# Channel-major projections of a two-block network: matmuls of 512 and 256 columns issued two and two over two blocks

## The chip, the cores and the metric

The kernel is one program on one core of a Trainium2 chip. The metric is the device time of one execution in microseconds, taken as the median of several runs; lower is better.

## The reference, cut to what matters

Two transformer-like blocks work on 256 tokens of width 2048 in float32. The first has gated recurrence and attention heads and a gated feed-forward net of width 5632 with a short convolution; the second has two layers with pooling, block attention, and attention into 256 memory tokens. Nearly all of the arithmetic lies in the projections, each a product of activations with a weight matrix:

```python
proj = h @ w_in[l]                                        # 2048 x 7176
x = x + jnp.concatenate([o_a, o_b], axis=-1) @ w_out[l]   # 2048 x 2048
x = x + (jax.nn.silu(conv(h @ w_gate)) * (h @ w_up)) @ w_down
mk, mv = jnp.split(mem @ w_mem_kv, 2, axis=-1)
k, v = jnp.split(h @ w_kv, 2, axis=-1)
u = h @ w_in[i]
y = mixed @ w_out[i]
pooled_mixed = jnp.einsum('bsgc,gcd->bsgd', pooled, pool_w)
```

## The kernel before

**Split operands.** Each float32 operand is split in two: a high part, rounded to TensorE's faster 32-bit format (fp32r), and a low part, the rest. A projection is the sum of high weight times high activation, high weight times low activation, and low weight times high activation. Activations lie as `[128, blocks of 128 channels, 2, 256 tokens]`, high beside low, in `ahl` (most projections), `hhl` (feed-forward down), `memhl` (memory), `fox_span` (half of the first output projection) and `phl` (pooling).

**Weight tiles.** Each projection is a phase: a number of chunks, each of `tpc` weight tiles. SP loads a tile (mostly 1 MB) into one of four `raw` buffers; ScalarE writes its high part into one of three slots of `hl_ring` (`hi`, L337) and VectorE its low part (`lo`, L340), two tiles ahead of TensorE. TensorE waits for a tile's low part (`lo_ready`), issues all its matmuls, and the last one raises `tile_used`, which frees the slot.

**Form A, channel-major.** The weights are the stationary operand, 128 by 128. For each block of 128 input channels there are two matmuls into the same bank of the accumulator `G`: L386 has the high weights and all 512 columns (high and low activations side by side), L387 has the low weights and the 256 columns of the high activations. Each has a weight load of its own. A chunk owns a pair of banks of `G`, one bank (512 float32) for each of two blocks of 128 output channels. A standard tile (`std_mats`) holds eight input blocks for both output blocks: 16 pairs of matmuls, the eight of output block 0 first, then the eight of block 1. A tile of the down projection (`down_mats`) has one output block and eleven input blocks; one of the pooling projection (`pool_mats`) has one output block and three.

**Form F, token-major.** The activations are stationary, the weights stream with 512 columns, and three matmuls (L391, L392, L393) of 512 columns follow one another. The diff does not alter what they issue. A further matmul stream stands at L881: the forget gate's projection, 48 matmuls of 256 columns, each with its own weight load.

**What sets the order.** The program is written engine by engine. `pe_phase` walks over chunks and tiles. `between` puts other work (transposes, attention heads, recurrence) behind a tile. VectorE and ScalarE read `G` when a chunk's last tile is done, and free the pair of banks with `pair_free`.

Of the kernel before, what the change touches and what calls it, by code (L numbers as in the profile page):

```python
# [25 lines left out]
P = 128  # L26
TOK = 256
# [37 lines left out]
def program(nc, A):  # L65
    ctx = ExitStack()
    with ctx:
# [44 lines left out]
        hi, lo = hl_ring[:, :, 0, :], hl_ring[:, :, 1, :]  # L112
# [40 lines left out]
        G = ctx.enter_context(nc.psum_tensor("G", [P, 4, 512], F32))  # L153
# [161 lines left out]
        order = list(phases.values())  # L315
# [39 lines left out]
        def no_evict(c):  # L355
            pass

        def pe_phase(eng, name, between=None, norm=None, halves=None):


            p = phases[name]
            xhl = p.rhs
            for c in range(p.chunks):
                pair = (p.chunk0 + c) % 2
                for t in range(p.tpc):
                    m = c * p.tpc + t
                    n = p.tile0 + m
                    s = n % RINGS
                    eng.wait_ge(lo_ready, n + 1)
                    if norm is not None and c == 0:  # L370
                        eng.wait_ge(n_lo, 4 * norm + (t + 1) * (4 // p.tpc))
                    if halves is not None and c == 0:
                        for ready, count in halves[t]:
                            eng.wait_ge(ready, count)
                    if t == 0 and p.chunk0 + c >= 2:
                        eng.wait_ge(pair_free[pair], (p.chunk0 + c) // 2)
                    if name.startswith("down") and c == 0 and t < 2:
                        eng.wait_ge(h_lo, HB // 2 * int(name[-1]) + (6 if t == 0 else 11))
                    last = None
                    for b, ks, width, col, first, final in p.mats(c, t):  # L380
                        bank = 2 * pair + b
                        for q, (kt, k) in enumerate(ks):
                            st, sp = first and q == 0, final and q == len(ks) - 1
                            if p.form == "A":
                                w = slice(kt * width + col, kt * width + col + P)
                                eng.matmul(G[:, bank, :], hi[:, s, w], xhl(k), start=st, stop=False)  # L386
                                last = eng.matmul(G[:, bank, 0:TOK], lo[:, s, w], xhl(k)[:, 0, :], start=False, stop=sp)  # L387
                            else:
                                w = slice(kt * width, (kt + 1) * width)
                                tok = slice(b * P, (b + 1) * P)  # L390
                                eng.matmul(G[:, bank, :], xhl(k)[:, 0, tok], hi[:, s, w], start=st, stop=False)  # L391
                                eng.matmul(G[:, bank, :], xhl(k)[:, 0, tok], lo[:, s, w], start=False, stop=False)  # L392
                                last = eng.matmul(G[:, bank, :], xhl(k)[:, 1, tok], hi[:, s, w], start=False, stop=sp)  # L393
                    last.then_inc(tile_used, 1)
                    if between is not None:
                        between(m)
# [432 lines left out]
        def _(pe):  # L829
# [25 lines left out]
            def x_transposes(m):  # L855
# [4 lines left out]
                for g in range(3 * m - 3, min(3 * m, 8)):  # L860
                    transposes(xtok, g)

            pe_phase(pe, "mem_k0", between=x_transposes)
            pe.wait_ge(vec_loaded, 11 * 16)
            pe.wait_ge(x_ready, 5)
            for v, n in enumerate((124, 105, 88)):
                last = pe.transpose(XP[0][:, v * P:v * P + n], vrows[0:n, v, :], ident[0:n, 0:n])
            last.then_inc(vec_t, 1)
            pe.wait_ge(x_ready, 8)
            pe_phase(pe, "mem_v0")  # L870
            pe_norm(pe, 0)
            for n in ("mem_k1", "mem_v1"):
                pe_phase(pe, n)
# [797 lines left out]
```

## Time and profile before

| | us |
|---|---|
| median of 3 runs | 2169.74 |
| lowest, highest | 2167.94, 2171.20 |
| the profiled execution | 2165.34 |
| its span, first to last instruction | 2163.6 |

The profile shows one execution. Its busy table gives each engine's time and share of the span. The chain that ended last is followed back from the last instruction. Groups of instructions are named by line, engine and operation with the tensors that they write and read. The timeline lists instructions by start time. A table of stretches counts the instructions of one line in given stretches of the span. PE is TensorE's matmul side, PEld its weight loads, DVE VectorE, ACT ScalarE. The mean granted TensorE clock is 0.979 of full speed.

### The profile page before, as it was taken

Reading aid. Unit: us, or ns where it says so; the run is one execution under the profiler, and the core shown is the slowest. Engines: PE = TensorE matmul, PEld = TensorE weight load, DVE = VectorE, ACT = ScalarE, POOL = GpSimd, SP = SyncE. Lnnn points to the kernel's source line nnn. Section 1 sums busy time; section 2 is a strip of 40 time slices with the busy share of each in tenths; the row PEclk is TensorE's granted clock in tenths of the full one; section 3 lists DMA queues with packets and bytes.
Section 4 is the critical chain, followed back from the end, with each engine's and each line's share of the span. In section 5 each row is a group of like instructions: output and inputs, shape, how many; then the busy total and the mean of one; then the engine's idle time right before and its main releaser. Section 6 shows DMA issues by size and latency. Waiting matters only on the chain.

```text
span 2163.6 us, 26132 instructions
## 1 busy us (share of the span) xinstructions
PE 2065.9 (95%) x11431; PEld 1787.2 (83%) x11431; DVE 1282.9 (59%) x1136; ACT 882.4 (41%) x785; POOL 32.2 (1%) x54
## 2 busy tenths in 40 slices
PE   7999999999799999999999997999889699999996
PEld 6888898888688888888888886888678588888885
DVE  4556555456666665556666555577576653566664
ACT  5435434444444443334444334333343334344532
POOL 1000000000000000000000000000000200000001
PEclk9999999999999999999999999999999899999998
DMA  8565544445445555675555666556175355654551
GB/s 276 175 219 189 172 140 156 156 137 175 156 156 195 195 194 149 186 224 181 194 178 178 163 185 192 156 176 199 40 230 185 97 188 181 189 155 138 195 195 59
DMA packets 381261, 373.38 MB, mean 173 GB/s; under 512 B 6526, under 2 KB 351419, under 8 KB 380123
## 3 DMA queue, kind: packets, MB, share of 16 engines
q1 hardware_dynamic: 379744, 365.19, 53.7%
q0 software_dynamic: 944, 6.36, 0.8%
q8 instruction: 90, 1.47, 0.3%
q10 hardware_dynamic: 459, 0.16, 0.0%
q14 instruction: 24, 0.20, 0.0%
HBM read 367.49 MB, written 4.19 MB: 172 GB/s over the span
## 4 chain that ended last, share of the span: by engine, by line
PE 92%; DVE 4%; ACT 1%; issue 1%; DMA 0%; POOL 0%; SPq 0%; DVEq 0%; ACTq 0%
PE G L386 49%; PE G L387 25%; PE G L391 4%; PE G L392 4%; PE G L393 4%; PE SB L605 2%; PE TB L503 1%; DVE hl_ring L340 1%; PE OB L626 1%; DMA raw<-in_w_mem_kv 0%; DVE xres L560 0%; ACT hl_ring L337 0%; DVE scr L401 0%; PE OB L629 0%; PE TB L881 0%
## 5 line engine op out<-in xcount | busy, mean ns | idle before, releaser
L386 PE MATMUL G<-ahl,hl_ring 128*128 128x512 f32 x3648 | 1293.3, 399 | 38.0 <-issue 31.9
L340 DVE TENSOR_TENSOR hl_ring<-raw,hl_ring 128x2048 fp32r<-128x2048 f32 (+2 forms) x372 | 787.5, 2121 | 520.6 <-ACT hl_ring L337 519.2
L387 PE MATMUL G<-ahl,hl_ring 128*128 128x256 f32 x3648 | 1023.7, 281 | 0.0
L337 ACT ACTIVATE hl_ring<-raw 128x2048 fp32r<-128x2048 f32 (+2 forms) x372 | 659.8, 1777 | 635.9 <-PE G L387 518.9
L386 PEld LDWEIGHTS G<-ahl,hl_ring 128*128 128x128 f32 x3648 | 688.8, 189 | 204.9 <-issue 36.1
L387 PEld LDWEIGHTS G<-ahl,hl_ring 128*128 128x128 f32 x3648 | 692.0, 190 | 0.4 <-issue 0.2
L386 PE MATMUL G<-hhl,hl_ring 128*128 128x512 f32 x704 | 248.8, 399 | 0.0
L387 PE MATMUL G<-hhl,hl_ring 128*128 128x256 f32 x704 | 197.7, 281 | 0.0
L386 PEld LDWEIGHTS G<-hhl,hl_ring 128*128 128x128 f32 x704 | 132.3, 188 | 33.0
L387 PEld LDWEIGHTS G<-hhl,hl_ring 128*128 128x128 f32 x704 | 133.0, 189 | 0.0
L391 PE MATMUL G<-hl_ring,ahl 128*128 128x512 f32 x256 | 100.2, 392 | 0.0
L393 PE MATMUL G<-hl_ring,ahl 128*128 128x512 f32 x256 | 99.7, 389 | 0.0
L392 PE MATMUL G<-hl_ring,ahl 128*128 128x512 f32 x256 | 99.7, 389 | 0.0
L401 DVE TENSOR_REDUCE arena<-G 128x512 f32<-128x1024 f32 x58 | 70.9, 1222 | 41.4 <-PE G L387 41.3
L1162 ACT ACTIVATE cbuf<-gsum,convp 128x256 f32<-128x256 f32 x44 | 24.1, 595 | 108.4 <-DVEq L1467 108.4
L641 ACT ACTIVATE ringscr<-SB,nmax 128x256 f32<-128x256 f32 (+1 forms) x48 | 20.2, 426 | 114.5 <-DVE nmax L662 114.5
L1168 ACT ACTIVATE hhl<-hv 128x512 fp32r<-128x512 f32 x22 | 13.9, 633 | 111.6 <-DVE hv L1483 111.6
L393 PEld LDWEIGHTS G<-hl_ring,ahl 128*128 128x128 f32 x256 | 48.1, 188 | 10.0
L391 PEld LDWEIGHTS G<-hl_ring,ahl 128*128 128x128 f32 x256 | 48.1, 188 | 9.8
L392 PEld LDWEIGHTS G<-hl_ring,ahl 128*128 128x128 f32 x256 | 48.1, 188 | 9.7
L386 PE MATMUL G<-memhl,hl_ring 128*128 128x512 f32 x128 | 47.1, 410 | 5.4 <-DVE hl_ring L340 5.4
L386 PE MATMUL G<-fox_span,hl_ring 128*128 128x512 f32 x128 | 45.7, 399 | 0.0
(306 smaller groups left out, 1499.7 us busy)
## 6 DMA issues: line engine op xcount, KB each, us to landing
raw<-in_w_in SPq DMA_DIRECT2D x120, 1024.0 KB, 5.5
raw<-in_w_out SPq DMA_DIRECT2D x48, 1024.0 KB, 5.4
raw<-in_w_ffn_gate SPq DMA_DIRECT2D x44, 1024.0 KB, 5.0
raw<-in_w_ffn_up SPq DMA_DIRECT2D x44, 1024.0 KB, 5.1
raw<-in_w_ffn_down SPq DMA_DIRECT2D x64, 704.0 KB, 4.9
raw<-in_w_kv_shared SPq DMA_DIRECT2D x24, 1024.0 KB, 5.1
raw<-in_w_mem_kv SPq DMA_DIRECT2D x16, 1024.0 KB, 7.7
raw<-in_pool_w SPq DMA_DIRECT2D x12, 192.0 KB, 2.5
```

What stands on the lines that cost most here:

```text
L337: eng.activation(hi[:, s, 0:size], raw[:, r, 0:size], ACT.Copy).then_inc(hi_ready, 1)
L340: eng.tensor_tensor(lo[:, s, 0:size], raw[:, r, 0:size], hi[:, s, 0:size].bitcast(F32), ALU.subtract).then_inc(lo_ready, 1)
L386: eng.matmul(G[:, bank, :], hi[:, s, w], xhl(k), start=st, stop=False)
L387: last = eng.matmul(G[:, bank, 0:TOK], lo[:, s, w], xhl(k)[:, 0, :], start=False, stop=sp)
L391: eng.matmul(G[:, bank, :], xhl(k)[:, 0, tok], hi[:, s, w], start=st, stop=False)
L392: eng.matmul(G[:, bank, :], xhl(k)[:, 0, tok], lo[:, s, w], start=False, stop=False)
L393: last = eng.matmul(G[:, bank, :], xhl(k)[:, 1, tok], hi[:, s, w], start=False, stop=sp)
L401: return eng.tensor_reduce(dst, g, AX.X, ALU.add)
L503: last = eng.matmul(TB[:, 0:TOK], meanw[:, :], normt[:, k, :], start=k == 0, stop=k == KT - 1)
L605: last = eng.matmul(o_, l_, r_, start=m == 0, stop=m == len(mm) - 1)
L626: eng.matmul(OB[:, 0:256], H.v(h, 0), pt[:, 0:256], start=True, stop=False)
L1162: act.activation(cbuf[:, b, :], gsum[:, b, :], ACT.Identity, scale=convp[:, f, 2:3], bias=convp[:, f, 3:4]).then_inc(conv_c, 1)
```

## The change

In form A the loop over output blocks outside and input blocks inside is replaced by one list. With two output blocks in the tile the list goes over the input blocks outside and the two output blocks inside; with one it goes over the input blocks. The list is taken two entries at a time: first the two L386 kinds (512 columns, high weights), then the two L387 kinds (256 columns, low weights). Where the list has an odd length (down: 11, pool: 3), the last entry stands alone. The number of matmuls and loads, their operands and the waits are the same. Form F is untouched.

```diff
+        def alternate(eng, p, pair, s, c, t):
+
+            mats = p.mats(c, t)
+            last = None
+            if len(mats) == 2:
+                order = [(mats[b], q) for q in range(len(mats[0][1])) for b in (0, 1)]
+            else:
+                order = [(mats[0], q) for q in range(len(mats[0][1]))]
+            for g in range(0, len(order), 2):
+                for (b, ks, width, col, first, final), q in order[g:g + 2]:
+                    kt, k = ks[q]
+                    w = slice(kt * width + col, kt * width + col + P)
+                    eng.matmul(G[:, 2 * pair + b, :], hi[:, s, w], p.rhs(k), start=first and q == 0, stop=False)
+                for (b, ks, width, col, first, final), q in order[g:g + 2]:
+                    kt, k = ks[q]
+                    w = slice(kt * width + col, kt * width + col + P)
+                    last = eng.matmul(G[:, 2 * pair + b, 0:TOK], lo[:, s, w], p.rhs(k)[:, 0, :], start=False,
+                                      stop=final and q == len(ks) - 1)
+            return last
+
...
-                    for b, ks, width, col, first, final in p.mats(c, t):
+                    if p.form == "A":
+                        last = alternate(eng, p, pair, s, c, t)
+                    for b, ks, width, col, first, final in p.mats(c, t) if p.form != "A" else ():
                         bank = 2 * pair + b
                         for q, (kt, k) in enumerate(ks):
                             st, sp = first and q == 0, final and q == len(ks) - 1
-                            if p.form == "A":
-                                w = slice(kt * width + col, kt * width + col + P)
-                                eng.matmul(G[:, bank, :], hi[:, s, w], xhl(k), start=st, stop=False)
-                                last = eng.matmul(G[:, bank, 0:TOK], lo[:, s, w], xhl(k)[:, 0, :], start=False, stop=sp)
-                            else:
+                            if p.form == "F":
                                 w = slice(kt * width, (kt + 1) * width)
```

## Rows read from the trace of the kernel before

**Rows 1.** Page, busy time: engine, busy us, share of span, instructions.
```profile
PE 2065.9 (95%) x11431; PEld 1787.2 (83%) x11431; DVE 1282.9 (59%) x1136; ACT 882.4 (41%) x785; POOL 32.2 (1%) x54
```
**Rows 2.** Page, chain that ended last: shares of the span by line.
```profile
PE G L386 49%; PE G L387 25%; PE G L391 4%; PE G L392 4%; PE G L393 4%; PE SB L605 2%; PE TB L503 1%; DVE hl_ring L340 1%; PE OB L626 1%; DMA raw<-in_w_mem_kv 0%; DVE xres L560 0%; ACT hl_ring L337 0%; DVE scr L401 0%; PE OB L629 0%; PE TB L881 0%
```
**Rows 3.** Waits of TensorE: who for whom, us in total, times, longest.
```profile
PE G L386 <- DVE hl_ring L340: 14.0, 5, 5.4
```
**Rows 4.** TensorE groups: out<-in, shape, count | busy, mean ns | idle before.
```profile
L386 PE MATMUL G<-ahl,hl_ring 128*128 128x512 f32 x3648 | 1293.3, 399 | 38.0 <-issue 31.9 <-DVE hl_ring L340 4.1 <-DVE ahl L1549 1.7
L387 PE MATMUL G<-ahl,hl_ring 128*128 128x256 f32 x3648 | 1023.7, 281 | 0.0
L386 PE MATMUL G<-hhl,hl_ring 128*128 128x512 f32 x704 | 248.8, 399 | 0.0
...
L386 PE MATMUL G<-memhl,hl_ring 128*128 128x512 f32 x128 | 47.1, 410 | 5.4 <-DVE hl_ring L340 5.4
L386 PE MATMUL G<-fox_span,hl_ring 128*128 128x512 f32 x128 | 45.7, 399 | 0.0
...
L386 PE MATMUL G<-pooledhl,hl_ring 128*128 128x512 f32 x36 | 15.7, 463 | 6.9 <-DVE hl_ring L340 4.5 <-DVE arena L1523 2.4
```
**Rows 5.** Timeline, TensorE, from 300.02 us: start us, duration us, instruction.
```profile
300.02 0.39 PE L386 MATMUL G<-ahl,hl_ring 128*128 128x512 f32 x1
300.25 0.27 PE L387 MATMUL G<-ahl,hl_ring 128*128 128x256 f32 x1
300.36 0.40 PE L386 MATMUL G<-ahl,hl_ring 128*128 128x512 f32 x1
...
303.83 0.40 PE L386 MATMUL G<-ahl,hl_ring 128*128 128x512 f32 x1
```
**Rows 6.** Timeline, TensorE, from 1000.00 us.
```profile
1000.00 0.40 PE L386 MATMUL G<-ahl,hl_ring 128*128 128x512 f32 x1
1000.23 0.28 PE L387 MATMUL G<-ahl,hl_ring 128*128 128x256 f32 x1
1000.35 0.40 PE L386 MATMUL G<-ahl,hl_ring 128*128 128x512 f32 x1
...
1004.24 0.40 PE L386 MATMUL G<-ahl,hl_ring 128*128 128x512 f32 x1
```
**Rows 7.** Stretches, L386 alone: length, PE and PEld busy (count), clock, DMA share, GB/s.
```profile
133.00:210.00 77.00, 77.00 (x219) 40.96 (x218) 1.00 0.63 205
...
478.00:582.00 104.00, 101.90 (x288) 53.99 (x288) 1.00 0.58 189
601.00:842.00 241.00, 241.00 (x696) 130.31 (x695) 1.00 0.56 182
846.00:1334.00 488.00, 488.00 (x1383) 259.51 (x1382) 1.00 0.63 189
1360.00:1534.00 174.00, 174.00 (x494) 92.51 (x493) 1.00 0.55 169
1593.00:1675.00 82.00, 82.00 (x238) 44.26 (x237) 1.00 0.60 193
1713.00:1772.00 59.00, 59.00 (x172) 31.86 (x171) 1.00 0.63 206
1843.00:1892.00 49.00, 49.00 (x140) 26.01 (x140) 1.00 0.64 193
```
**Rows 8.** Timeline, TensorE, token-major form, first and last of twelve matmuls.
```profile
229.94 0.39 PE L391 MATMUL G<-hl_ring,ahl 128*128 128x512 f32 x1
...
232.43 0.39 PE L393 MATMUL G<-hl_ring,ahl 128*128 128x512 f32 x1
```
**Rows 9.** Timeline, TensorE, gate projection, first and last of 22 matmuls.
```profile
211.92 0.40 PE L881 MATMUL TB<-ahl,fwhi 128*128 128x256 f32 x2
...
214.44 0.28 PE L881 MATMUL TB<-ahl,fwhi 128*128 128x256 f32 x1
```
**Rows 10.** Timeline, TensorE's weight loads, at 300.02 us.
```profile
300.02 0.19 PEld L387 LDWEIGHTS G<-ahl,hl_ring 128*128 128x128 f32 x1
```

## The prediction

> **What bounds the kernel now.** I read the busy table first. TensorE is busy for 95% of the span, VectorE, the next engine, for 59% [rows 1]. The chain that ended last says the same: 49% and 25% of the span go to the two matmul lines that the change reorders, L386 (512 columns) and L387 (256 columns), and none of the lines of another engine that it lists reaches 2% [rows 2]. The waits of TensorE agree: its largest wait on another engine for these matmuls is for the low half of a weight tile, 14.0 us in five waits over the whole span [rows 3]. So nothing but the distance from one matmul's start to the next sets most of the time, and a nanosecond saved on each lands in the end almost whole.
>
> There are 3648 + 704 + 128 + 128 + 36 = 4644 pairs of one L386 and one L387 [rows 4]. The mean durations in those rows (399 and 281 ns) are no price: matmuls overlap, and a duration holds the pipeline's latency. What counts is start to start, so I went to the timeline.
>
> **Two paces of the same pair.** From 300.02 to 303.83 us there are 11 pairs: 3.81 / 11 = 346.4 ns a pair, some 230 ns from the 512 to the 256 and some 115 ns back to the next 512 [rows 5]. From 1000.00 to 1004.24 us the same two lines take 4.24 / 12 = 353.3 ns a pair [rows 6]. Which pace holds is a matter of the stretch, and it persists. I read stretches in which hardly anything but these pairs runs, each length divided by its number of matmuls (weight loads, one fewer where a matmul is cut by the edge) [rows 7]. The granted clock is 1.00 in all eight, the full level of 2.4 GHz, so the clock is not what differs: 241 us / 695 = 346.8 ns, 82 / 237 = 346.0 and 59 / 171 = 345.0 are the quick pace; 77 / 218 = 353.2, 488 / 1382 = 353.1, 174 / 493 = 352.9, 104 / 288 (with 2 us idle, 101.9 / 288 = 353.8) and 49 / 140 = 350.0 are the slow one. (An edge is worth one pair, which blurs the short ones.) The difference is 353.1 - 346.8 = 6.3 ns by the two long stretches and 6.9 ns by the two timelines; I take 6.6 ns and call it a step.
>
> The slow stretches hold 219 + 1383 + 494 + 288 + 140 = 2524 pairs, the quick ones 696 + 238 + 172 = 1106. The remaining 1014 lie between transposes and attention matmuls; I put half of them, 507, to the slow pace (my choice, the timeline shows both there). That makes 3031 slow pairs, 65% of all, and 3031 x 6.6 ns = 20.0 us in steps. This is all that a reordering can win if the quick pace is the floor.
>
> Is it? Where matmuls of one size follow one another, each with a weight load of its own, the rows show one pace only. The token-major form of 512 columns: 229.94 to 232.43 us, 11 distances, 226.4 ns [rows 8]. The gate projection of 256 columns: 211.92 to 214.44 us, 21 distances, 120.0 ns [rows 9]. Their sum is 346.4 ns, exactly the quick pair. So the quick pace is the sum of the two kinds, and the step appears in mixed streams only.
>
> **The change, part by part.** It removes and adds no instruction: 4644 matmuls of each kind, the same loads, the same operands, waits and increments, on one core. Only TensorE's order within a weight tile changes, from 512, 256, 512, 256 to 512, 512, 256, 256 over the two output blocks.
>
> (a) New neighbours. 512 after 512: 226.4 ns by rows 8; 256 after 256: 120.0 ns by rows 9. One 512 to 256 and one 256 to 512 stay: 230 to 235 and 115 to 120 ns [rows 5, 6]. Four matmuls come to 226.4 + 120.0 + 346.4 = 692.8 ns at the quick pace and 226.4 + 120.0 + 353.3 = 699.7 ns at the slow one, against 692.8 and 706.6 ns now. Nothing is won where the pace is quick; one step of two is won where it is slow.
>
> (b) How many size changes are left. Tiles with two blocks: (4644 - 704 - 36) / 2 = 1952 groups of four. The down projection has one block and 11 matmul pairs a tile (704 / 11 = 64 tiles), taken two by two with one left over: 6 changes for 11, so 384. Pool: 12 tiles of three, 24. Together 2360 for 4644. At today's slow share, 0.65 x 2360 = 1540 steps stay and 3031 - 1540 = 1491 go: 1491 x 6.6 ns = 9.8 us.
>
> (c) Weight loads. In the trace a load starts with the matmul before the one it serves: one is at 300.02 us, with the matmul of 300.02 [rows 5, 10]. Now a load under a 256 serves a 512; afterwards one load in four lies under a 256 and serves a 256. Two 256s in a row with a load each are what rows 9 show at 120.0 ns, so the term is 0 in (a). Bounds: the quick pair's 256 takes about 115 ns, so -5 ns; above, a full step, +6.6 ns on each of 2322 groups, 15 us. I take 0, the nearest row being the same kind of operation.
>
> (d) Accumulator banks. Successive matmuls now write different banks. Today a tile changes bank once, after 8 pairs. The tile of rows 5 ends soon after 303.83, so its change falls near 301.4, within the 11 pairs whose mean is 346.4 ns: no cost seen, and the 11 distances of rows 8 in one bank are no cheaper. I take 0; upper bound one step per matmul pair again.
>
> (e) Other engines. A tile's last matmul still releases it and both banks of a chunk are still released together, so SP's transfers, ScalarE's high halves and VectorE's low halves keep their order. A tile of 16 pairs takes 16 x 0.3533 = 5.65 us of TensorE and would take some 5.60; VectorE at 59% has room for that. The cover of the weight tiles stays.
>
> [...]
>
> Sum: -9.8 us. The profiled execution took 2165.3 us, of which 1.7 lie outside its span; the median of the runs shown is 2169.7, 4.4 us more. I take the 9.8 off the median: 2159.9 us, -0.45%.
>
> **The rivals.** Count steps per group of four; today it is 3031 / 2322 = 1.3.
> - Forecast: the step belongs to a size change and keeps its share, 0.65 per group. 2159.9 us. For: one-size streams show none. Chance 0.34.
> - All gone: the step needs the strict alternation to hold itself, and the new pattern settles at the quick pace everywhere. -20.0 us, 2149.7 us. For: the paces last for hundreds of us, like a rhythm that locks, and a new rhythm might not lock. Against: no row shows a mixed stream in fours. Chance 0.20.
> - Order is indifferent: the step comes once per pair or its like, whatever the neighbours, or every group takes exactly one. 0 us (2169.7) in the first case, 2322 x 6.6 = 15.3 in place of 20.0, so -4.7 us (2165.0), in the second. For: the quick pair is a plain sum. Chance 0.26.
> - Slower: the new rhythm locks in the slow pace everywhere, two steps a group, the second one at the 256 that follows a 256 into another bank, where a load and a change of bank fall together in the shortest slot, some 0.12 us. (4644 - 3031) x 6.6 = +10.6 us, 2180.4 us. It decides from 1.3 steps a group on. For: after short interruptions today's stream falls into the slow pace more often than not, five of the eight stretches in the table [rows 7]. Against: rows 9. Chance 0.20.
>
> **How the numbers follow.** The predicted time is the forecast's, 2159.9 us. About 0.2% (4.3 us) is what a measurement of this kernel can tell from no change. Forecast and "all gone" are faster, 0.54. The case of -4.7 us lies on that bound and I count it with "order is indifferent", 0.26. With a little of the slower case that is too small to be told, within 0.2% comes to 0.27 and slower to 0.19. For 8 in 10 the range starts at the case "all gone" with 1.7 us beyond for the choice of 507, 2148, and runs through the forecast (alone: 2155 to 2164) and the indifferent order into two thirds of the slower case, 2177.
>
> **What would show it.** Timeline after: two L386 starts 0.23 us apart, then 0.23, then 0.12, 0.12; groups of four at 0.693 or 0.700 us, not 0.707. Long stretches of such groups, length over number of L386: 346.4 to 350 ns. If all stretches read 346.7, "all gone" holds; if 353, the rhythm locked slow; if a mixture of 346.7 and 353.3 stays with the old share, order is indifferent. In (c), a distance of 256 to 256 well over 120 ns would refute the load term; in (d), 512 to 512 over 227 ns the bank term. What makes the prediction wrong otherwise: the down projection or the stretches between attention matmuls choosing another pace than today, which is worth up to 507 x 6.6 = 3.3 us here.

## The result and the profile after

The changed kernel takes 2155.07 us (median of 4 runs, 2154.10 to 2156.07) against 2169.36 us before in the same comparison: ratio 0.9934, 95% interval 0.9916 to 0.9951. That is 14.3 us less, where 9.8 us were forecast. The profiled execution took 2154.1 us with a span of 2152.4 us, 11.2 us less than the span before.

The page of the changed kernel, busy time, then the chain that ended last by line:

```profile
PE 2052.7 (95%) x11431; PEld 1779.1 (83%) x11431; DVE 1282.6 (60%) x1136; ACT 882.2 (41%) x785; POOL 32.2 (1%) x54
...
PE G L370 49%; PE G L374 24%; PE G L409 4%; PE G L411 4%; PE G L410 4%; PE SB L623 2%; PE TB L521 1%; DVE hl_ring L340 1%; PE OB L644 1%; ACT hl_ring L337 0%; DVE xres L578 0%; DVE scr L419 0%; PE TB L899 0%; DVE arena L501 0%; PE OB L647 0%
```

L370 and L374 are the old L386 and L387. Counts, the other engines' busy times and the chain's make-up are those of [rows 1, 2]; TensorE alone has become shorter. Its largest wait on another engine for these matmuls has not moved either (14.0 us in [rows 3]):

```profile
PE G L370 <- DVE hl_ring L340: 14.7, 5, 5.0
```

So the gain lies between the starts of the matmuls. The timeline of TensorE in the changed kernel, same place as [rows 6] (a line with x2 is two matmuls, start of the first and length of both):

```profile
1000.16 0.63 PE L370 MATMUL G<-ahl,hl_ring 128*128 128x512 f32 x2
1000.63 0.39 PE L374 MATMUL G<-ahl,hl_ring 128*128 128x256 f32 x2
1000.86 0.63 PE L370 MATMUL G<-ahl,hl_ring 128*128 128x512 f32 x2
...
1005.73 0.40 PE L370 MATMUL G<-ahl,hl_ring 128*128 128x512 f32 x1
```

Eight groups of four from 1000.16 to 1005.73 us: 5.57 / 8 = 0.696 us, or 348.1 ns per pair. Before it was 353.3 here and 346.4 in the stretches of [rows 5]. The stretches agree; L370 alone, length, PE and PEld busy with counts, clock, DMA share, GB/s:

```profile
133.00:210.00 77.00, 69.39 (x223) 33.65 (x222) 1.00 0.65 205
478.00:575.00 97.00, 87.32 (x278) 42.23 (x279) 1.00 0.61 195
601.00:842.00 241.00, 217.28 (x694) 105.34 (x692) 1.00 0.58 183
1000.00:1200.00 200.00, 180.32 (x575) 87.39 (x575) 1.00 0.57 183
```

Each length is divided by the mean of its two counts: 97 / 278.5 = 348.3, 241 / 693 = 347.8, 200 / 575 = 347.8, 77 / 222.5 = 346.1 ns per pair, with an uncertainty of one or two pairs at the edges, since matmuls of one size now come in twos (for the shortest stretch that is 1.6 to 3.1 ns). What was slow (133, 478, 1000) and what was quick (601) now run at one pace, close to 348.1. The two paces of the old kernel have become one, some 1.5 ns above its quick one and 5 ns below its slow one.

### The profile page after: what moved, and what is told of

It reads as the page before. It is cut to its first block, busy times and chain, and to the rows that moved or that the text cites. A ratio compares the mean times of both kernels' runs of the same rounds, so it can differ in the third digit from the quotient of the medians.

```text
span 2152.4 us, 26132 instructions
## 1 busy us (share of the span) xinstructions
PE 2052.7 (95%) x11431; PEld 1779.1 (83%) x11431; DVE 1282.6 (60%) x1136; ACT 882.2 (41%) x785; POOL 32.2 (1%) x54
## 4 chain that ended last, share of the span: by engine, by line
PE 93%; DVE 4%; ACT 2%; issue 1%; POOL 1%; DVEq 0%; ACTq 0%; POOLq 0%
PE G L370 49%; PE G L374 24%; PE G L409 4%; PE G L411 4%; PE G L410 4%; PE SB L623 2%; PE TB L521 1%; DVE hl_ring L340 1%; PE OB L644 1%; ACT hl_ring L337 0%; DVE xres L578 0%; DVE scr L419 0%; PE TB L899 0%; DVE arena L501 0%; PE OB L647 0%
## 5 line engine op out<-in xcount | busy, mean ns | idle before, releaser
L370 PE MATMUL G<-ahl,hl_ring 128*128 128x512 f32 x3648 | 1156.7, 399 | 38.8 <-issue 31.9
L374 PEld LDWEIGHTS G<-ahl,hl_ring 128*128 128x128 f32 x3648 | 689.3, 189 | 163.5
L374 PE MATMUL G<-ahl,hl_ring 128*128 128x256 f32 x3648 | 720.2, 279 | 0.0
L370 PEld LDWEIGHTS G<-ahl,hl_ring 128*128 128x128 f32 x3648 | 559.8, 190 | 41.9 <-issue 35.7
L370 PE MATMUL G<-hhl,hl_ring 128*128 128x512 f32 x704 | 223.5, 395 | 0.0
L374 PEld LDWEIGHTS G<-hhl,hl_ring 128*128 128x128 f32 x704 | 132.3, 188 | 28.6
L374 PE MATMUL G<-hhl,hl_ring 128*128 128x256 f32 x704 | 144.0, 279 | 0.0
L370 PEld LDWEIGHTS G<-hhl,hl_ring 128*128 128x128 f32 x704 | 109.8, 189 | 2.7
L370 PE MATMUL G<-memhl,hl_ring 128*128 128x512 f32 x128 | 42.3, 413 | 5.0 <-DVE hl_ring L340 5.0
L419 DVE TENSOR_REDUCE hv<-G 128x512 f32<-128x1024 f32 x22 | 26.9, 1225 | 30.3 <-PE G L374 30.3
```

The lines of the kernel that those rows point to most:

```text
L370: eng.matmul(G[:, 2 * pair + b, :], hi[:, s, w], p.rhs(k), start=first and q == 0, stop=False)
L374: last = eng.matmul(G[:, 2 * pair + b, 0:TOK], lo[:, s, w], p.rhs(k)[:, 0, :], start=False, stop=final and q == len(ks) - 1)
L419: return eng.tensor_reduce(dst, g, AX.X, ALU.add)
```

## The experiments

The table has the kernels that were executed six or ten times, each with its own spread. The kernel before stands once for each comparison. The other kernels below were executed once. All code edits are cut to the lines that matter (`...`).

| kernel | runs | median us | lowest to highest | ratio to before, 95% interval |
|---|---|---|---|---|
| before, with the first four | 31 | 2167.16 | 2153.62 to 2172.30 | |
| twos in one bank | 10 | 2154.32 | 2152.45 to 2157.29 | 0.9951 (0.9934 to 0.9969) |
| alternating sizes, banks in turn | 10 | 2163.65 | 2154.89 to 2174.41 | 0.9988 (0.9963 to 1.0013) |
| fours | 10 | 2164.16 | 2163.15 to 2165.58 | 1.0002 (0.9981 to 1.0022) |
| whole tile | 10 | 2153.87 | 2152.22 to 2155.07 | 0.9961 (0.9943 to 0.9980) |
| before, with the next two | 19 | 2166.04 | 2153.98 to 2173.03 | |
| one group of twos, then alternating | 10 | 2170.05 | 2168.01 to 2171.82 | 1.0024 (1.0003 to 1.0044) |
| skewed | 10 | 2173.16 | 2171.42 to 2175.00 | 1.0031 (1.0016 to 1.0047) |
| before, with the last | 11 | 2165.71 | 2154.19 to 2171.58 | |
| tiles turned | 6 | 2150.14 | 2148.51 to 2150.97 | 0.9933 (0.9908 to 0.9957) |

**Sizes or banks?** The change does two things at once: it puts equal sizes side by side, and it lets successive matmuls write different banks. Two kernels do one alone. The first keeps the groups of four but takes them within one output block:

```diff
-            if len(mats) == 2:
-                order = [(mats[b], q) for q in range(len(mats[0][1])) for b in (0, 1)]
-            else:
-                order = [(mats[0], q) for q in range(len(mats[0][1]))]
+            order = [(mat, q) for mat in mats for q in range(len(mat[1]))]
...
```

> Edit: the groups of four (512, 512, 256, 256) are kept, but taken over two input blocks of one output block, so that all four write one bank; banks change once per tile, as before the change. Theory S (the order of the sizes sets the pace): as the changed kernel, ratio 0.993 to 0.994, some 348.4 ns per pair everywhere. Theory B (the gain comes from writing two banks in turn): the old two paces, 346.7 and 353.3 ns, ratio 0.999 to 1.001.

Measured: 2154.32 us, the changed kernel's time. Its timeline has five groups of four from 1099.90 to 1103.38 us, 3.48 / 5 = 0.696 us each:

```profile
1099.90 0.39 PE L371 MATMUL G<-ahl,hl_ring 128*128 128x256 f32 x2
1100.13 0.62 PE L367 MATMUL G<-ahl,hl_ring 128*128 128x512 f32 x2
...
1103.38 0.40 PE L371 MATMUL G<-ahl,hl_ring 128*128 128x256 f32 x2
```

The second alternates the sizes as before and alternates the banks with each pair:

```diff
...
-            for g in range(0, len(order), 2):
+            for g in range(0, len(order), 1):
...
```

Each slice `order[g:g + 2]` becomes `order[g:g + 1]`; in the kernels below it grows with the step in the same way.

> Edit: sizes alternate 512, 256, 512, 256 as before the change, but the two output blocks take turns pair by pair, so that the bank changes with each pair. Theory S: ratio 0.998 to 1.002, two paces of 346.7 and 353.3 ns as before. Theory B: ratio about 0.994 and one pace near 348.4 ns.

Measured: 2163.65 us, not told apart from before; the interval of the ratio, 0.9963 to 1.0013, leaves out the 0.994 of theory B. Both old paces are there, but they have changed places; L367 alone, in stretches:

```profile
133.00:210.00 77.00, 76.89 (x222) 41.62 (x222) 1.00 0.65 205
...
601.00:842.00 241.00, 241.00 (x683) 128.15 (x682) 1.00 0.57 180
```

241 / 682 = 353.4 ns where [rows 7] have the quick pace, and 77 / 222 = 346.8 ns where they have the slow one. Theory S holds against theory B: the order of the sizes does it, and no effect of the banks is seen. That the same phases have the other pace in this kernel also shows that the pace doesn't belong to a phase's own weights and activations.

**Do fewer size changes help further?**

```diff
-            for g in range(0, len(order), 2):
+            for g in range(0, len(order), 4):
...
```

> Edit: four matmuls of 512 columns, then four of 256, over two input blocks and two output blocks. Theory S1 (each change of size carries a fixed share of a step; 3.3 ns per group in the changed kernel): 2 x 693.3 + 3.3 ns per eight, 347.5 ns per pair, 4 us less than the changed kernel, ratio about 0.9915. Theory L (each order of sizes locks into a pace of its own, with no rule by the number of changes): any pace between 346.7 and 353.3 ns.

Measured: 2164.16 us, 9 us more than in twos. Groups of eight in its timeline:

```profile
1100.49 1.09 PE L367 MATMUL G<-ahl,hl_ring 128*128 128x512 f32 x4
1101.42 0.63 PE L371 MATMUL G<-ahl,hl_ring 128*128 128x256 f32 x4
...
1104.69 1.09 PE L367 MATMUL G<-ahl,hl_ring 128*128 128x512 f32 x4
```

Three groups in 4.20 us: 350.0 ns per pair in this stretch. Half as many size changes cost more, so theory S1, a fixed share of a step at each change, is refuted. The spread, 2.4 us over ten executions, is small like the changed kernel's. With threes:

> Edit, on the changed kernel: three matmuls of 512 columns, then three of 256, over two output blocks. If the cost grows steadily from twos (348.4 ns per pair) to fours (350.8): 349 to 350 ns, device time 2157 to 2162 us. Theory L without a rule: any pace from 346.7 to 353.3.

Measured: 2164.52 us (one run), above the 2157 to 2162 expected from a steady rise. Three matmuls of 512 and three of 256 take 1.04 to 1.07 us, never twice the same, and a single pair stands at the end of a tile of 16:

```profile
1101.19 0.88 PE L367 MATMUL G<-ahl,hl_ring 128*128 128x512 f32 x3
...
1105.41 0.86 PE L367 MATMUL G<-ahl,hl_ring 128*128 128x512 f32 x3
```

Twelve pairs in 4.22 us are 351.7 ns each. With all of a tile's matmuls of one size in a row:

```diff
-            for g in range(0, len(order), 2):
+            for g in range(0, len(order), 16):
...
```

> Edit: all matmuls of 512 columns of a weight tile (16; 11 in the down projection), then all of 256. One change of size each way per tile. Theory S1: 346.4 to 346.9 ns per pair, 7 to 8 us less than the changed kernel, ratio about 0.990. Theory L: any pace between 346.7 and 353.3 ns; the token-major phases and the gate projection, streams of one size, ran at 226.4 and 120.0 ns, and if these hold here as well the stretches are 16 x 226.4 and 16 x 120.0 ns long.

Measured: 2153.87 us, 1.2 us under the changed kernel's 2155.07 (whose runs are from another comparison), not 7 to 8. Its timeline shows where the rest went:

```profile
1001.27 3.82 PE L367 MATMUL G<-ahl,hl_ring 128*128 128x512 f32 x16
1004.93 2.08 PE L371 MATMUL G<-ahl,hl_ring 128*128 128x256 f32 x16
1006.84 3.82 PE L367 MATMUL G<-ahl,hl_ring 128*128 128x512 f32 x16
```

A tile takes 5.57 us, 348.1 ns a pair. The sixteen 512s take 3.66 us, where 16 x 226.7 is 3.63 (226.7 ns is the distance in the run with one size only, below; [rows 8] give 226.4); the sixteen 256s take 1.91 us, where 16 x 120.0 is 1.92. The seventh 512 of the tile starts here:

```profile
1002.66 0.39 PE L367 MATMUL G<-ahl,hl_ring 128*128 128x512 f32 x1
```

The first six distances take 1.39 us, 232 ns each, and the ten behind them 2.27 us, 227 ns each. So long runs of one size do settle at the paces of [rows 8, 9], and what a tile takes above them lies in the first 512s after 256s.

**Is it the weight load under the short matmul?** Two kernels change the length of the low-weight matmul in the kernel before.

```diff
-                                last = eng.matmul(G[:, bank, 0:TOK], lo[:, s, w], xhl(k)[:, 0, :], start=False, stop=sp)
+                                g2 = G[:, bank, :].rearrange("p (h t) -> p h t", h=2)[:, :, 0:192]
+                                last = eng.matmul(g2, lo[:, s, w], xhl(k)[:, :, 0:192], start=False, stop=sp)
```

> Edit, on the kernel before: the low-weight matmul streams 384 columns (192 tokens of the high and of the low activations) in place of 256; order 512, 384, 512, 384. It leaves out 64 tokens of the low-weight product and adds a low-times-low term. Theory W (the step is a weight load that doesn't quite fit under a matmul of 256 columns): one pace, (512 + 384) / 2.4 + 2 x 13.3 = 400.0 ns per pair in all stretches. Theory L (a rhythm of the order of sizes, whatever is loaded): more than one pace or one off 400.0 by a step of 6.7 ns or a part of it.

Measured: 2440.34 us. There are two paces, 4.07 / 10 = 407.0 ns per pair around 150 us and 4.13 / 10 = 413.0 ns around 1100 us, and neither is 400.0. (The 400.0 is an estimate: no run has 384 columns alone, and 173.3 ns lie halfway between 120.0 for 256 and 226.7 for 512.)

```profile
149.96 0.39 PE L386 MATMUL G<-ahl,hl_ring 128*128 128x512 f32 x1
150.19 0.34 PE L388 MATMUL G<-ahl,hl_ring 128*128 128x384 f32 x1
...
154.03 0.39 PE L386 MATMUL G<-ahl,hl_ring 128*128 128x512 f32 x1
...
1099.86 0.40 PE L386 MATMUL G<-ahl,hl_ring 128*128 128x512 f32 x1
1100.09 0.34 PE L388 MATMUL G<-ahl,hl_ring 128*128 128x384 f32 x1
...
1103.99 0.40 PE L386 MATMUL G<-ahl,hl_ring 128*128 128x512 f32 x1
```

The stride of those operands could have been the cause, so it was repeated with contiguous columns:

```diff
...
+                                    last = eng.matmul(G[:, bank, 0:384], lo[:, s, w],
+                                                      xhl(k).rearrange("p h t -> p (h t)")[:, 0:384], start=False, stop=sp)
```

> Edit, on the kernel before: the low-weight matmul streams 384 contiguous columns (the high activations of 256 tokens, then the low ones of 128), in place of 256; in the first output projection it stays at 256. It adds part of the low-times-low term. It repeats the run with 192 + 192 columns without its stride. If the stride made the two paces there (406.7 and 413.3 ns): 400.0 ns. If the two sizes did: 406.7 and 413.3 again.

Measured: 2430.51 us, with both paces again: ten pairs from 149.73 to 153.80 us, 407 ns each, and ten from 1099.63 to 1103.77 us, 414 ns each:

```profile
149.73 0.39 PE L386 MATMUL G<-ahl,hl_ring 128*128 128x512 f32 x1
...
153.80 0.39 PE L386 MATMUL G<-ahl,hl_ring 128*128 128x512 f32 x1
...
1099.63 0.40 PE L386 MATMUL G<-ahl,hl_ring 128*128 128x512 f32 x1
...
1103.77 0.40 PE L386 MATMUL G<-ahl,hl_ring 128*128 128x512 f32 x1
```

The stride is not the cause. A load under 384 columns has some 53 ns more than one under 256, and the two paces are still there, 6 to 7 ns apart. Theory W as the cause of the step is refuted. The other direction:

```diff
+                                n2 = TOK if sp else P
+                                last = eng.matmul(G[:, bank, 0:n2], lo[:, s, w], xhl(k)[:, 0, 0:n2], start=False, stop=sp)
```

> Edit, on the kernel before: the low-weight matmul streams 128 columns (half the tokens; the other half of the low-weight product is left out, except in the last matmul of a block); order 512, 128. Theory W: the load that stands under the 128 shows in full, and the distance after it stays at 113 to 120 ns, so that a pair takes 340 to 350 ns and nothing is won. Theory L: loads are not the limit, (512 + 128) / 2.4 + 2 x 13.3 = 293.3 ns per pair, give or take a step of 6.7.

Measured: 2121.19 us, 49 us less than the 2169.98 us that the kernel before took beside it (one execution each). TensorE's matmuls and loads:

```profile
1049.74 0.44 PE L386 MATMUL G<-ahl,hl_ring 128*128 128x512 f32 x1
1050.02 0.22 PE L388 MATMUL G<-ahl,hl_ring 128*128 128x128 f32 x1
1050.02 0.19 PEld L386 LDWEIGHTS G<-ahl,hl_ring 128*128 128x128 f32 x1
1050.08 0.44 PE L386 MATMUL G<-ahl,hl_ring 128*128 128x512 f32 x1
1050.13 0.19 PEld L388 LDWEIGHTS G<-ahl,hl_ring 128*128 128x128 f32 x1
1050.36 0.22 PE L388 MATMUL G<-ahl,hl_ring 128*128 128x128 f32 x1
1050.36 0.19 PEld L386 LDWEIGHTS G<-ahl,hl_ring 128*128 128x128 f32 x1
...
1051.44 0.44 PE L386 MATMUL G<-ahl,hl_ring 128*128 128x512 f32 x1
```

Five pairs in 1.70 us, 340 ns. Half of the columns of the low matmul are gone (53 ns, half of what a 512 takes more than a 256), and the pair is only 6 ns shorter than the quick pair of [rows 5], 13 ns shorter than the slow one. By the loads the pair divides into 0.11 us (1050.02 to 1050.13) and 0.23 us (1050.13 to 1050.36); 340 - 226.7 is 113 ns. The matmuls start otherwise: the 128 comes 0.28 us after the 512 and the next 512 only 0.06 us after the 128. So the least that a short matmul adds to the pair is some 113 ns, and the rhythm of the loads says that the load is the limit; that reading is argued from these rows, since no run has the short matmul without its load. W is right about the floor, which lies just under the 120 ns of a matmul of 256, and wrong about the step. Only one pace was seen here; L386 alone, in a stretch, gives 200 / 587.5 = 340.4 ns:

```profile
1000.00:1200.00 200.00, 200.00 (x588) 109.97 (x587) 1.00 0.59 186
```

The Trainium skill, page "TensorE: Matmul & The Clock Gate", section "LDWEIGHTS (loading the stationary operand)", gives a load as its columns over 1.2 GHz, by estimate 107 ns for these 128; the 113 ns lie 6 ns above it.

**One size only.**

```diff
-                                last = eng.matmul(G[:, bank, 0:TOK], lo[:, s, w], xhl(k)[:, 0, :], start=False, stop=sp)
+                                last = eng.matmul(G[:, bank, :], lo[:, s, w], xhl(k), start=False, stop=sp)
```

> Edit, on the kernel before: the low-weight matmul streams all 512 columns (it adds the low-times-low term). Only one size is left in these stretches. All theories by which the step needs two sizes: 2 x 226.7 = 453.3 ns per pair, everywhere, in one pace. If the step belongs to the channel-major form itself (these weights, these operands), a second pace of 460 ns appears.

Measured: 2637.04 us; seven starts, six distances in 1.36 us, 226.7 ns each (the matmuls of 512 columns in both lines):

```profile
1050.05 0.39 PE L386 MATMUL G<-hhl,hl_ring 128*128 128x512 f32 x1
...
1051.41 0.39 PE L386 MATMUL G<-hhl,hl_ring 128*128 128x512 f32 x1
```

No second pace of 460 ns per pair shows in the stretches that were read. The step needs two sizes; the channel-major form has none of its own.

**What picks the pace of an alternating stretch?** The times of the kernel before range over 19 us, from 2153.62 to 2172.30 in 31 executions, while every kernel in groups stays within 5 us. The kernel with alternating sizes and banks in turn ranges over 19.5 us. The clock doesn't explain it: the three shortest of all its executions (2153.62 to 2153.98 us) and the three longest (2172.02 to 2173.03 us) have mean granted clocks of 0.978 to 0.980 alike. Nor does the traffic of transfers tell the paces apart: [rows 7] have the quick one at 182 to 206 GB/s and the slow one at 169 to 205. If each execution picks its paces anew at the interruptions, a fixed start for each tile should narrow the range. Two kernels do that; the first begins each tile with one group of twos and then alternates:

```diff
+            plan = [(False, 0), (False, 1), (True, 0), (True, 1)]
+            plan += [(low, i) for i in range(2, len(order)) for low in (False, True)]
...
```

> Edit, on the changed kernel: only the first four matmuls of each weight tile go 512, 512, 256, 256; the other 14 pairs alternate 512, 256 (output blocks in turn). The question is what picks the pace of an alternating stretch. Theory P (a disturbance at the stretch's start picks it, and it then holds): every tile starts alike, so all tiles of one kind have one pace, and the time varies from run to run much less than that of the kernel before. If it is the quick one, 346.7 to 347.1 ns per pair and 2147 to 2150 us, better than both kernels; if the slow one, 353 ns and some 2175 us. Theory N (the pace is set by something outside TensorE's stream): both paces as before, ratio 0.999 to 1.001.

The second starts with two of 512, alternates 512 and 256, and ends with two of 256:

```diff
+            plan = [(False, 0)]
+            for i in range(1, len(order)):
+                plan += [(False, i), (True, i - 1)]
+            plan.append((True, len(order) - 1))
...
```

> Edit, on the changed kernel: a tile starts with two of 512, then 256 and 512 alternate, and it ends with two of 256. Theory P: again one pace for all tiles, and little variation from run to run; quick 2147 to 2150 us, slow some 2175 us. Theory N: both paces, ratio 0.999 to 1.001.

Measured: 2170.05 us within 3.8 us, and 2173.16 us within 3.6 us, at the top of the range of the kernel before. L376 and L378 alone, 1000 to 1200 us; the first row is that of the seeded kernel,

```profile
1000.00:1200.00 200.00, 197.54 (x568) 104.20 (x567) 1.00 0.58 186
```

the second that of the skewed one:

```profile
1000.00:1200.00 200.00, 197.28 (x567) 103.97 (x566) 1.00 0.59 186
```

200 / 567.5 = 352.4 and 200 / 566.5 = 353.0 ns: the slow pace, and in the first the timeline from 1061.14 to 1064.67 us (ten pairs, 353 ns) shows it between two seeds. This is what theory P foretold: with a fixed start for each tile there is one pace and a small spread. Both seeds gave the slow one, and two orders are few: a seed that gives the quick pace was not found, and it isn't shown that the interruptions of the kernel before act in the same way.

**A version that beats both.** The whole-tile kernel pays around its size changes. If every second tile of a chunk issues its 256s first, a tile has one change in place of two (`high` and `low` list the tile's matmuls of 512 and of 256 columns):

```diff
+            turned = t % 2 == 1 and p.name != "pool"
+            plan = low + high if turned else high + low
...
```

> Edit, on the run with a whole tile's sizes in a row: every second tile of a chunk issues its 256s first and its 512s after (pooling excepted), so that a tile holds one change of size and its neighbour begins with the size that it ended with. Theory L with a price per disturbance: the whole-tile run settled at 226.7 and 120.0 ns and paid some 20 ns per tile around its two changes, 308 tiles, 6 us; half of the changes gives 3 us less than that run, some 2151 us, and little variation from run to run. If the price belongs to the tile's boundary or to the bank change instead: no gain over 2154 us.

Measured: 2150.14 us, 2148.51 to 2150.97, ratio 0.9933.

```profile
1000.65 7.44 PE L378 MATMUL G<-ahl,hl_ring 128*128 128x512 f32 x32
1007.93 4.00 PE L375 MATMUL G<-ahl,hl_ring 128*128 128x256 f32 x32
1011.76 7.44 PE L378 MATMUL G<-ahl,hl_ring 128*128 128x512 f32 x32
```

Two tiles take 11.11 us, 347.2 ns a pair against 348.1 in the whole-tile kernel. The median is 3.7 us under that kernel's and 4.9 us under the changed kernel's, and its range touches neither of theirs. The ratios do not separate it from either of the two, because each was made with other executions of the kernel before, which move by several us. The traces do: 0.9 ns on each of 4644 pairs are 4.2 us.

## Why the prediction was right, and where it was not

The time (2155.07 us) lies in the range and at the very edge of the forecast's own 2155 to 2164, the direction is right and the size is of the order forecast. That it comes so near is in part luck, as the second and the last of these points say. By its steps:

- **Bound and price of a step** held. TensorE's start-to-start distance is the bound; nothing else moved. Other engines took no part in the gain (e).
- **The share that stays** was the wrong picture with nearly the right sum. I let 0.65 steps per group stay, as today's mixture of quick and slow stretches, and expected groups of 0.693 or 0.700 us. There is no mixture: groups take 0.696 us everywhere, half a step of 6.6 ns above the floor. In steps that is 0.5 x 2322 x 6.6 = 7.7 us left of 20.0, a gain of 12.3 us. The span fell by 11.2, the sum said 9.8. The share that I carried over, 0.65 steps a group, and the half step that came have different causes and are near by chance.
- **"The step belongs to a size change"** is refuted. Fours have half of the changes and cost 9 us more than twos. The step belongs to the whole order of sizes: each order has its pace, and strict alternation has two.
- **Terms (a) and (c)**, the distances of equal neighbours taken from one-size streams, are right for long runs of one size (whole tile, all 512). In groups of four they don't hold: over the eight groups of the timeline the two 512s take 0.465 us and the two 256s 0.231, where one-size distances give 0.453 and 0.240; only the sum comes near, 3 ns over. The bounds of -5 ns and one step held that. The floor of 113 ns in the run with 128 columns lies just under a matmul of 256.
- **Term (d)**, banks at no cost, is borne out: twos in one bank take 2154.32 us, and two 512s in a row last 0.62 to 0.63 us in its timeline as in the changed kernel's.
- **The rival "order is indifferent"** is refuted for this stream: twos take 348.1 ns a pair, fours 350.0, turned tiles 347.2, with the same matmuls and loads. The Trainium skill, page "TensorE: Matmul & The Clock Gate", section "Back-to-back issue gap", gives the gap of an isolated matmul at full clock as its columns over 2.4 GHz plus about 2.5 ns, by estimate 216 and 109 ns for these two sizes, and says that in a stream of loads and matmuls both set the spacing. It has no term for the order of sizes; here, with a load for each matmul, one-size streams take 226.7 and 120.0 ns, and the order moves a pair by up to 7 ns.
- **The rival "slower"**, a rhythm that locks slow everywhere, is no fancy: the two seeded kernels do just that and lie 0.24% and 0.31% above the kernel before. Its stated place, a 256 after a 256 into another bank, does not cost a full step, since the changed kernel has that neighbour in every group of four over two banks and takes half a step a group.
- **The median.** I took the sum off a median of three executions that stood 4.4 us above the profiled one, and held 0.2% to be what can be told from no change; the executions of the kernel before range over 0.9%. The changed kernel's median stands 1.0 us above its own, 2154.1. Of the 14.3 us, 11.2 are seen in the spans and the other 3.1 come from the old kernel's other executions being slower than the profiled one. The four of this comparison lie high: the 31 of the next have their median at 2167.16 us, against which the gain is 12.1 us, near the 12.3 of half a step a group. Its range of 19 us over 31 runs fits executions with more and with fewer slow stretches: 4644 pairs x 6.6 ns bound it at 31 us. That they pick so was argued from the spread and from the seeded kernels; only one execution of the old kernel was profiled.

What stays open: which clock or buffer makes the steps of 6.6 ns, why fours and threes are worse than twos, and why both seeds gave the slow pace. No run here tells.

## What to carry to other kernels

When one engine is busy throughout, read the distance from start to start of its instructions in several stretches, not the mean duration: two paces of the same code are time that a mere reordering can win, and a kernel whose runs spread far more than its variants' may be changing between such paces. Don't reason from "fewer changes of size is better": try the orders, since twos won 0.5 to 0.7%, fours nothing, and whole tiles with every second one turned had the lowest median. A fixed start for each tile may fix the wrong pace: both that were tried here fixed the slow one.

## What the runs showed of the hardware that was not expected

- The same alternating stream of matmuls of 512 and 256 columns, at the same granted clock of 1.00, runs at 346.4 or at 353.3 ns per pair and holds its pace over hundreds of us. With 512 and 384 columns it is 407 or 413 ns, both above the estimate of 400 ns from one-size distances. With 512 and 128 columns only one pace was seen, 340 ns, and with 512 alone 226.7 ns per matmul.
- After 256s, sixteen 512s take 3.66 us in place of 3.63: the first six distances are 232 ns, the others 227.
- Halving a matmul of 256 columns between two of 512 wins 6 ns of the 53 that its columns take; the short matmul still adds 113 ns to the pair, and the two loads start 0.11 and 0.23 us apart.
- Writing successive matmuls into two banks in turn or into one makes no difference that these executions can show: in twos 2154.3 us in one bank (10 executions) beside 2155.1 in two (4), and in strict alternation 2163.7 us with the banks in turn (10) beside 2167.2 (31), ratio 0.9963 to 1.0013.
